# Holding the last three depths of two projections by token tile, in a fused transformer layer

## The chip, the core and the metric

The kernel runs on one core of one Trainium2 chip. The metric is the device time of one execution in microseconds (us), as the median of several; less is better. All arithmetic that matters is float32 in quality: the large matrix products are made from split operands, as told below.

## The reference

One encoder layer over 256 tokens of width 2048. What is computed, cut to what matters:

```
h = rms_norm(x, pre_mix_g);  z = h @ w_in                # 2048 -> 7296
ya = neighbourhood_attention(...)   # 512 columns
yb = rwkv7_mixer(...)               # 768 columns, a recurrence in both directions
yc = retention_mixer(...)           # 768 columns
y = concatenate([ya, yb, yc]) @ w_out[l]                 # 2048 -> 2048   "output projection"
x = x + rms_norm(y, post_mix_g[l])
h = rms_norm(x, pre_mlp_g[l])                            # "second norm"
u = square(relu(h @ w_up[l])) @ w_down[l]                # 2048 -> 8192 -> 2048, "up" and "down projection"
x = x + rms_norm(u, post_mlp_g[l])
```

All inputs are float32.

## The kernel before

**Splitting.** Every operand of a large product is split in two: a rounded high part and the rest. A product is then three matmuls: high by high, low by high, and high by low. ScalarE makes the high part of a weight half (`hi`, L1217 to L1221), VectorE its rest (`lo`, L692 to L697). A *half* is 128 partitions by 1024 weights, 512 KB. Halves are numbered h through the whole kernel: the input projection's, then the output projection's from OUT_H (32 halves, two for each of 16 depths of 128 rows), the up projection's from UP_H, the down projection's from DOWN_H (128 halves, two for each of 64 depths), up to END_H.

**Buffers.** The sync engine fetches half h into one of 4 raw slots when the rest of half h - 4 is made (`fetch`, L489). The split parts lie in a ring of 3 slots (`w_hi`, `w_lo`, SPLIT = 3). Both `hi(h)` and `lo(h)` therefore wait for the semaphore `gemm_half` to reach h - 2, which says that TensorE has finished half h - 3. The arena is a large tensor of 32,896 words for each partition, which holds everything else and is cut up anew in each stage.

**The output and down projections (`rows`, L1957 to L1997).** The stationary operand is a block of activations (128 rows of depth by 128 tokens), the moving one 512 weights. All 8 banks of PSUM are the accumulators: 4 for token tile 0, 4 for token tile 1, two for each half of the 2048 columns. A *part* (t, j) is 6 matmuls of 512 columns: one depth, one token tile t, one half j. For each depth: wait for half 2n, part (1, 0), part (0, 0), wait for half 2n + 1, part (1, 1), part (0, 1). The last depth goes in the order (0, 0), (0, 1), (1, 0), (1, 1), and each part signals on its own (`quarter_done`), so that the norm behind it can begin.

**The norm behind each of the two.** For each token tile and half ScalarE squares and sums (`half_squares`, L1498), and VectorE multiplies by the gain (`gained`, L1121); then come the root, its reciprocal, and two additions to x (`add_half`, L1136), each with its own signal. After the output projection those additions write `x1` (signal `x1_ready`), after the down projection the result, which goes out in 4 transfers.

**The second norm's blocks (`turned`, L1566; `split_h`, L685 on VectorE and L1210 on ScalarE).** x1 is transposed by TensorE in 16 blocks of two 128 by 128 transposes each, one block to a bank, in 6 banks; TensorE begins when three of the four additions are done (`least = 2 * TT - 1`). ScalarE makes the high part of a block out of PSUM, VectorE the rest, and from the seventh block on TensorE waits for the rest of the block six before. After all 32 transposes the up projection begins; depth kt of its first tile waits for the rest of block kt. The root of the second norm itself is applied after the up projection, from sums that ScalarE makes of x1.

**The down projection's activations.** ScalarE makes the high part of the activations of depth m (`u_split(m)`), then `hi` of its two halves. VectorE makes their rest (`u_rest(m)`), then `lo` of the two halves. TensorE waits for `ulo_done` of depth m before depth m.

**Before the output projection.** The mixers run in `turn(i)` for six retention heads; the first also finishes the recurrence's output: `summed_recurrence` (L1009) adds, `gated_recurrence` (L1014) multiplies, 128 by 1536 each. `gap()` is a place where the running input projection's work is put in: on TensorE its matmuls, on the others splits that they need. Then ScalarE copies 16 blocks of the mixed activations to their high parts (`head_of`) and VectorE makes their rests (`rest_of`). Both do blocks 0 and 1 first, then half OUT_H + 2, then all 14 other blocks in one go, and only then the further halves.

What sets the order: each engine has its own program written out by hand as above, and semaphores between them. Nothing is reordered at run time but by these waits.

## Time and profile before

| | us |
|---|---|
| median of 3 runs (1385.03 to 1386.26) | 1385.25 |
| the profiled execution, its own time | 1388.11 |
| span of its trace, first to last instruction | 1386.3 |
| TensorE busy (96%) | 1326.4 |
| VectorE busy (61%) | 840.1 |
| ScalarE busy (47%) | 646.0 |
| mean granted TensorE clock | 0.989 of full speed |

The 1.8 us between the span and the profiled execution's own time lie before the first and behind the last instruction. In the rows below, a timeline row is: start, duration, engine, line, operation, what it writes and reads, how many instructions are merged, and in square brackets the idle time before it with what ended it. PEld is TensorE's weight load. TensorE's matmul durations overlap one another, so the pace is read from the starts.

### The profile page before, as it was taken

The numbers are of one execution on the slowest core, as the hardware profiler recorded it, in microseconds if no ns is written. First come the engines' busy times: TensorE is split into PE (matmuls) and PEld (weight loads), VectorE is DVE, ScalarE is ACT, GpSimd is POOL, SyncE is SP. The second block draws the span as 40 slices with busy tenths as digits, with TensorE's granted clock in tenths as the row PEclk, the third lists the DMA queues.
The fourth block names the chain that finished last, engine by engine and source line by source line (L and its number), as shares of the span: only waits on it lengthen the run. The fifth ranks groups of instructions, "written<-read, shape, count | busy, mean of one in ns | idle before, by whom it ended". The sixth has DMA issues, their size and how long they took to land.

```text
span 1386.3 us, 25418 instructions
## 1 busy us (share of the span) xinstructions
PE 1326.4 (96%) x10537; PEld 1159.5 (84%) x10537; DVE 840.1 (61%) x1167; ACT 646.0 (47%) x983; POOL 299.2 (22%) x231
## 2 busy tenths in 40 slices
PE   6999999999999899898999999999999999999996
PEld 5999888888888899686888888888888888888885
DVE  5566788888876665545654554455455554555555
ACT  5465554455334345535544444444444444444443
POOL 0010223233315011000155555444440000000000
PEclk9999999999999999999999999999999999999999
DMA  8656333223339334485576666666666666666663
GB/s 246 185 163 189 104 90 93 78 78 92 102 99 213 92 107 120 139 285 155 147 218 183 185 188 189 184 186 190 185 185 194 197 191 192 195 195 191 192 196 122
DMA packets 285751, 226.50 MB, mean 163 GB/s; under 512 B 15237, under 2 KB 263301, under 8 KB 284741
## 3 DMA queue, kind: packets, MB, share of 16 engines
q1 hardware_dynamic: 285168, 223.64, 55.1%
q8 instruction: 83, 1.36, 0.4%
q0 software_dynamic: 240, 1.18, 0.3%
q14 instruction: 32, 0.25, 0.1%
q10 hardware_dynamic: 228, 0.07, 0.0%
HBM read 222.76 MB, written 2.10 MB: 162 GB/s over the span
## 4 chain that ended last, share of the span: by engine, by line
PE 84%; DVE 8%; ACT 5%; issue 2%; ACTq 0%; DVEq 0%
PE psum L1965 31%; PE psum L1605 17%; PE psum L1606 9%; PE psum L1594 7%; PE psum L1595 6%; PE psum L1596 6%; DVE w_lo L696 2%; PE psum L1734 1%; PE psum L1720 1%; ACT w_hi L1221 1%; DVE arena L865 1%; PE psum L1924 1%; PE psum L1811 0%; PE psum L1572 0%; PE psum L1932 0%
## 5 line engine op out<-in xcount | busy, mean ns | idle before, releaser
L696 DVE TENSOR_TENSOR w_lo<-raw,w_hi 128x1024 fp32r<-128x1024 f32 x402 | 505.4, 1260 | 444.4 <-ACT w_hi L1221 443.5
L1221 ACT ACTIVATE w_hi<-raw 128x1024 fp32r<-128x1024 f32 x402 | 424.5, 1059 | 489.5 <-PE psum L1965 233.2
L1605 PE MATMUL psum<-act_both,w_hi 128*128 128x512 f32 x1024 | 362.1, 399 | 0.0
L1965 PE MATMUL psum<-w_hi,act_both 128*128 128x512 f32 x1280 | 344.8, 391 | 5.7 <-DVE w_lo L696 2.6
L1965 PEld LDWEIGHTS psum<-w_hi,act_both 128*128 128x128 f32 x1280 | 240.5, 188 | 57.2 <-DVE w_lo L696 3.0
L1606 PE MATMUL psum<-act_both,w_lo 128*128 128x256 f32 x1024 | 287.6, 281 | 0.0
L1594 PE MATMUL psum<-act_both,w_hi 128*128 128x256 f32 x912 | 274.0, 300 | 3.9 <-DVE w_lo L696 2.4
L1595 PE MATMUL psum<-act_both,w_hi 128*128 128x256 f32 x912 | 259.8, 285 | 0.0
L1596 PE MATMUL psum<-act_both,w_lo 128*128 128x256 f32 x912 | 259.7, 285 | 0.0
L1605 PEld LDWEIGHTS psum<-act_both,w_hi 128*128 128x128 f32 x1024 | 192.4, 188 | 48.1 <-DVE w_lo L696 0.2
L1965 PE MATMUL psum<-w_lo,act_both 128*128 128x512 f32 x640 | 197.5, 390 | 0.0
L1606 PEld LDWEIGHTS psum<-act_both,w_lo 128*128 128x128 f32 x1024 | 193.4, 189 | 0.0
L1594 PEld LDWEIGHTS psum<-act_both,w_hi 128*128 128x128 f32 x912 | 176.2, 193 | 12.9 <-issue 5.2
L1595 PEld LDWEIGHTS psum<-act_both,w_hi 128*128 128x128 f32 x912 | 176.5, 194 | 0.3
L1596 PEld LDWEIGHTS psum<-act_both,w_lo 128*128 128x128 f32 x912 | 176.4, 193 | 0.0
L1965 PEld LDWEIGHTS psum<-w_lo,act_both 128*128 128x128 f32 x640 | 120.5, 188 | 25.1
L647 POOL TENSOR_TENSOR arena<-arena 128x512 f32<-128x512 f32 x32 | 42.4, 1325 | 304.8 <-DVE arena L1164 304.8
L650 POOL TENSOR_SCALAR arena<-arena 128x512 f32<-128x512 f32 x32 | 74.0, 2312 | 2.8
L652 POOL TENSOR_TENSOR arena<-arena 128x512 f32<-128x512 f32 x32 | 64.1, 2003 | 2.7
L640 POOL TENSOR_TENSOR arena<-arena 128x256 f32<-128x256 f32 x12 | 14.4, 1225 | 83.7 <-DVE arena L1024 83.7
L555 POOL TENSOR_TENSOR arena<-arena 128x256 f32<-128x256 f32 x12 | 10.7, 915 | 95.9 <-ACT arena L1316 95.9
L621 POOL TENSOR_SCALAR arena<-arena,small 128x64 f32<-128x64 f32 x24 | 16.2, 689 | 70.2 <-DVE arena L910 43.5
(201 smaller groups left out, 1055.5 us busy)
## 6 DMA issues: line engine op xcount, KB each, us to landing
raw<-in_w_up SPq DMA_DIRECT2D x128, 512.0 KB, 4.0
raw<-in_w_down SPq DMA_DIRECT2D x128, 512.0 KB, 4.5
raw<-in_w_in SPq DMA_DIRECT2D x114, 512.0 KB, 4.2
raw<-in_w_out SPq DMA_DIRECT2D x32, 512.0 KB, 4.5
arena<-in_x SPq DMA_DIRECT2D x2, 1024.0 KB, 6.5
arena<-in_na_rpb SPq DMA_DIRECT2D x16, 128.0 KB, 4.6
arena<-in_x SPq DMA_DIRECT2D x1, 2048.0 KB, 8.4
out_x<-arena SPq DMA_DIRECT2D x4, 512.0 KB, 2.7
```

The costliest lines, as they stand in the source:

```text
L621: last = pool.tensor_scalar(state_dec[:, d], state[:, d], ec[q][:, d, c:c + 1], None, ALU.mult)
L647: pool.tensor_tensor(r, r, token_scale.unsqueeze(1).broadcast_to([P, 2, T]), ALU.mult).then_inc(s["up_scaled"], 1)
L650: pool.tensor_scalar(r, r, 0.0, None, ALU.max).then_inc(s["up_scaled"], 1)
L652: pool.tensor_tensor(u[:, 2 * q:2 * q + 2], r, r, ALU.mult).then_inc(s["relu_free"], 1)
L696: dve.tensor_tensor(w_lo[:, h % SPLIT], raw[:, h % RAW], w_hi[:, h % SPLIT].bitcast(F32), ALU.subtract).then_inc(s["lo_half"], 1)
L1221: act.activation(w_hi[:, h % SPLIT], raw[:, h % RAW], ACT.Copy).then_inc(s["hi_half"], 1)
L1594: pe.matmul(dst, wh, act_hi[:, kt], start=kt == 0, stop=False)
L1595: pe.matmul(dst, wh, act_lo[:, kt], start=False, stop=False)
L1596: last = pe.matmul(dst, wl, act_hi[:, kt], start=False, stop=kt == KT - 1)
L1605: pe.matmul(bank[b].rearrange("p (a t) -> p a t", a=2), wh, act_both[:, :, kt], start=kt == 0, stop=False)
L1606: last = pe.matmul(bank[b][:, 0:T], wl, act_hi[:, kt], start=False, stop=kt == KT - 1)
L1965: last = pe.matmul(bank[4 * t + 2 * j + b], lhs[:, tokens], w[:, h % SPLIT, b * 512:(b + 1) * 512], start=start, stop=stop)
```

## The change

The last HELD = 3 depths of the output and of the down projection are done by token tile: first all their parts of token tile 0, then all those of token tile 1, with the split weights of all six halves kept. For this the last four halves of each projection get split slots of their own (`spare`), cut from the end of the arena. A helper `slot_free` says what a half waits for. The second norm's first twelve blocks are transposed two to a bank, in the order NORM_ORDER; four of them are begun for token tile 0 before token tile 1 is there. At the start of the output projection a weight half's split alternates with two activation blocks. In the mixers the two recurrence operations stand at other places. The core of the diff:

```diff
+HELD = 3
+        def spare_slot(h):
+            for end in (UP_H, END_H):
+                if end - 2 * HELD + 2 <= h < end:
+                    return h - (end - 2 * HELD + 2)
+            return None
+        def slot_free(eng, h):
+            if spare_slot(h) is not None:
+                eng.wait_ge(s["gemm_half"], h - 2 * HELD - 2)
+                eng.wait_ge(s["y_lo"], KT)
+            elif UP_H <= h < UP_H + 2:
+                eng.wait_ge(s["held_free"], h - UP_H + 1)
+            elif h == UP_H + 2:
+                eng.wait_ge(s["gemm_half"], UP_H - 2 * HELD)
+            elif h >= SPLIT:
+                eng.wait_ge(s["gemm_half"], h - SPLIT + 1)
+        NORM_ORDER = [0, 3, 1, 4, 2, 5, 6, 7, 9, 10, 8, 11, 12, 13, 14, 15]
+        NORM_EARLY = NORM_ORDER[:4]
+        def norm_place(k):
+            if k < 12:
+                return bank[2 + k // 6 * 3 + k % 3][:, k % 6 // 3 * T:(k % 6 // 3 + 1) * T]
+            return bank[k - 11][:, 0:T]
+        def norm_mate(k):
+            if k >= 12:
+                return k
+            return k + 3 if k % 6 < 3 else k - 3
 ...
@@ VectorE @@
                 rotate(i)
+                if i == 0:
+                    summed_recurrence()
                 gap()
 ...
-                    if i == 0:
-                        summed_recurrence()
                     gap()
                     take_p(i, 1)
                     if more:
                         maxima(i + 1)
-                    if i == 0:
-                        gated_recurrence()
                     gap()
                 decayed(i)
                 gap()
+                if i == 0:
+                    gated_recurrence()
 ...
-            lo(OUT_H + 2)
-            for n in range(2, KT):
+            for n in range(2, KT, 2):
+                lo(OUT_H + 1 + n // 2)
                 rest_of(n)
-            for h in range(OUT_H + SPLIT, UP_H + 1):
+                rest_of(n + 1)
+            for h in range(OUT_H + 1 + KT // 2, UP_H):
                 lo(h)
 ...
-            rs = gained(0, 1)
+            rs = gained(0, 1, lambda: lo(UP_H))     # lo(UP_H) between the two multiplications
 ...
+            def split_x1(blocks):
+                for k in blocks:
+                    dve.wait_ge(s["h_hi"], KT + k + 1)
+                    dve.scalar_tensor_tensor(act_lo[:, k], norm_place(k), vect("g2")[:, k:k + 1],
+                                             act_hi[:, k].bitcast(F32), ALU.mult, ALU.subtract).then_inc(s["h_lo"], 1)
+            split_x1(range(HALF_KT))
             lo(UP_H + 1)
-            split_h(("g2", KT))
+            split_x1(range(HALF_KT, KT))
             lo(UP_H + 2)
-            for t in range(TT):
-                token_root(t)
+            token_root(0)
+            lo(UP_H + 3)
+            token_root(1)
@@ ScalarE @@
+            out_square(0, 0, 0)
+            out_square(0, 0, 1)
+            hi(UP_H)
+            out_square(0, 1, 0)
+            hi(UP_H + 1)
+            x1_square(0, 0)
+            out_square(0, 1, 1)
+            x1_square(0, 1)
+            for k in range(KT):
+                act.wait_ge(s["xt_done"], KT + max(NORM_ORDER.index(k), NORM_ORDER.index(norm_mate(k))) + 1)
+                if norm_mate(k) < k:
+                    act.wait_ge(s["h_lo"], KT + norm_mate(k) + 1)
+                act.activation(act_hi[:, k], norm_place(k), ACT.Copy, scale=vect("g2")[:, k:k + 1]).then_inc(s["h_hi"], 1)
+            hi(UP_H + 2)
+            x1_square(1, 0)
+            hi(UP_H + 3)
+            x1_square(1, 1)
+            hi(UP_H + 4)
@@ TensorE @@
+            def held_rows(depths):
+                for n, lhs_hi, lhs_lo in depths:
+                    final = n == depths[-1][0]
+                    for j in range(2):
+                        pe.wait_ge(s["lo_half"], 2 * n + j + 1)
+                        last = part(n, lhs_hi, lhs_lo, 0, j, final=final)
+                        if final:
+                            last.then_inc(s["quarter_done"], 1)
+                for j in range(2):
+                    for n, lhs_hi, lhs_lo in depths:
+                        final = n == depths[-1][0]
+                        last = part(n, lhs_hi, lhs_lo, 1, j, final=final)
+                        if n == depths[0][0]:
+                            last.then_inc(s["held_free"], 1)
+                        elif final and j == 0:
+                            last.then_inc(s["quarter_done"], 1)
+                        elif final:
+                            last.then_inc(s["gemm_half"], 2 * HELD)
 ...
-            turned(x1, KT, "x1_ready", 2 * TT - 1)
+            pe.wait_ge(s["x1_ready"], 2)
+            for k in NORM_EARLY:
+                turn_x1(k, 0)
+            pe.wait_ge(s["x1_ready"], 3)
+            for n, k in enumerate(NORM_ORDER):
+                if k == 9:
+                    pe.wait_ge(s["x1_ready"], 4)
+                if k > 12:
+                    pe.wait_ge(s["h_lo"], KT + norm_mate(k - 13) + 1)
+                if k not in NORM_EARLY:
+                    turn_x1(k, 0)
+                turn_x1(k, 1).then_inc(s["xt_done"], 1)
 ...
-            for m in range(FF_T):
+            for m in range(FF_T - HELD):
                 pe.wait_ge(s["ulo_done"], m + 1)
-                rows(DOWN_H // 2 + m, u_hi[:, m % U_RING], u_lo[:, m % U_RING], m == 0, m == FF_T - 1)
+                rows(DOWN_H // 2 + m, u_hi[:, m % U_RING], u_lo[:, m % U_RING], m == 0)
+            pe.wait_ge(s["ulo_done"], FF_T)
+            held_rows([(DOWN_H // 2 + m, u_hi[:, m % U_RING], u_lo[:, m % U_RING])
+                       for m in range(FF_T - HELD, FF_T)])
```

The output projection's depths 13 to 15 go through the same `held_rows`, behind a wait for all 16 activation blocks.

## Rows read from the trace of the kernel before

**Rows 1.** Waits of TensorE over the whole run: total, times, longest.

```profile
PE psum L1572 <- DVE arena L1138: 6.7, 1, 6.7
...
PE psum L1965 <- DVE w_lo L696: 2.6, 1, 2.6
PE psum L1594 <- DVE w_lo L696: 2.4, 2, 1.8
```

**Rows 2.** Timeline of VectorE in the first mixer turn.

```profile
466.38 1.23 DVE L696 TENSOR_TENSOR w_lo<-raw,w_hi 128x1024 fp32r<-128x1024 f32 x1 [1.64 <-ACT w_hi L1221]
...
468.18 1.75 DVE L1009 TENSOR_TENSOR arena<-arena 128x1536 f32<-128x1536 f32 x1
...
473.03 1.76 DVE L1014 TENSOR_TENSOR arena<-arena 128x1536 f32<-128x1536 f32 x1
474.71 1.22 DVE L696 TENSOR_TENSOR w_lo<-raw,w_hi 128x1024 fp32r<-128x1024 f32 x1
```

**Rows 3.** Timeline at the output projection's start: TensorE, VectorE, ScalarE.

```profile
570.51 1.22 PE L1965 MATMUL psum<-w_hi,act_both 128*128 128x512 f32 x2 [2.58 <-DVE w_lo L696]
...
564.54 4.78 DVE L1106 TENSOR_TENSOR act_both<-arena,act_both 128x256 fp32r<-128x256 f32 x14
569.23 3.49 DVE L696 TENSOR_TENSOR w_lo<-raw,w_hi 128x1024 fp32r<-128x1024 f32 x3
...
562.26 4.39 ACT L1486 ACTIVATE act_both<-arena 128x256 fp32r<-128x256 f32 x14
```

**Rows 4.** Stretches: length, engines' busy time (instructions), granted clock, DMA share, GB/s.

```profile
570.50:573.90 3.40, 3.39 (x8) 2.72 (x9) 2.22 (x2) 0.00 (x0) 0.00 (x0) 0.50 0.63 188
...
651.40:655.80 4.40, 0.00 (x0) 0.00 (x0) 4.27 (x5) 4.30 (x10) 0.00 (x0) 1.00 0.02 5
655.80:662.60 6.80, 4.56 (x20) 3.96 (x21) 6.70 (x11) 5.64 (x13) 0.00 (x0) 0.50 0.11 31
...
590.00:610.00 20.00, 20.00 (x90) 16.57 (x89) 9.54 (x8) 7.42 (x7) 0.00 (x0) 1.00 0.91 341
```

**Rows 5.** Timeline of all engines from the output projection's end to the up projection.

```profile
656.68 2.48 DVE L1138 SCALAR_TENSOR_TENSOR arena<-arena,small 128x1024 f32<-128x1024 f32 x2
...
658.01 2.43 PEld L1572 LDWEIGHTS psum<-cst,arena 128*128 128x128 f32 x12 [7.08 <-DVE arena L1138]
658.02 6.81 PE L1572 MATMUL psum<-cst,arena 128*128 128x128 f32 x32 [6.66 <-DVE arena L1138]
...
659.81 5.95 ACT L1214 ACTIVATE act_both<-psum,vec 128x256 fp32r<-128x256 f32 x16 [1.13 <-PE psum L1572]
660.32 6.36 DVE L689 SCALAR_TENSOR_TENSOR act_both<-psum,vec,act_both 128x256 fp32r<-128x256 f32 x16
...
664.38 0.20 PEld L1572 LDWEIGHTS psum<-cst,arena 128*128 128x128 f32 x2 [0.19 <-DVE act_both L689]
...
664.58 0.48 PE L1605 MATMUL psum<-act_both,w_hi 128*128 128x512 f32 x1
```

**Rows 6.** Timeline late in the down projection: one step of its pipeline.

```profile
1356.75 1.06 ACT L1221 ACTIVATE w_hi<-raw 128x1024 fp32r<-128x1024 f32 x1 [1.66 <-PE psum L1965]
...
1357.85 1.23 DVE L696 TENSOR_TENSOR w_lo<-raw,w_hi 128x1024 fp32r<-128x1024 f32 x1 [1.49 <-ACT w_hi L1221]
...
1358.99 0.42 DVE L1173 TENSOR_TENSOR act_both<-arena,act_both 128x256 fp32r<-128x256 f32 x1
```

**Rows 7.** Timeline of the kernel's end.

```profile
1373.11 1.03 ACT L1501 ACTIVATE arena<-psum 128x1024 f32<-128x1024 f32 x1
...
1374.26 1.23 DVE L1130 TENSOR_TENSOR arena<-psum,arena 128x1024 f32<-128x1024 f32 x1
...
1375.17 0.61 PE L1965 MATMUL psum<-w_hi,act_both 128*128 128x512 f32 x2
...
1380.69 2.48 DVE L1138 SCALAR_TENSOR_TENSOR arena<-arena,small 128x1024 f32<-128x1024 f32 x2
```

**Rows 8.** The page's DMA issues for one weight: count, KB each, us from issue to landing.

```profile
raw<-in_w_down SPq DMA_DIRECT2D x128, 512.0 KB, 4.5
```

More of the change, by code:

```diff
@@ L202, in layer @@
         ARENA = 32896
-        arena = sb("arena", [P, ARENA])
+        LATER = ARENA - 2 * (2 * HELD - 2) * HALF
+        arena = sb("arena", [P, LATER])
+        with nc.sbuf_tensor("arena_later", [P, ARENA - LATER], F32) as arena_later:
+            pass
+        spare = sb("spare", [P, 2, 2 * HELD - 2, HALF], F32R)
+        spare_hi, spare_lo = spare[:, 0], spare[:, 1]
         psum = ctx.enter_context(nc.psum_tensor("psum", [P, 8, 512], F32))
@@ L458, in backwards, with high, low @@
                            ap=steps[:-1] + [[-last, count]])
+        def spare_slot(h):
[3 more added lines that the diff above has]
+            return None
+        def high(h):
+            return w_hi[:, h % SPLIT] if spare_slot(h) is None else spare_hi[:, spare_slot(h)]
+        def low(h):
+            return w_lo[:, h % SPLIT] if spare_slot(h) is None else spare_lo[:, spare_slot(h)]
+        def slot_free(eng, h):
[18 more added lines that the diff above has]
+            return k + 3 if k % 6 < 3 else k - 3
         def raw_landed(eng, h):
@@ L1121, in out_half, with gained @@
                 return psum[:, 4 * t + 2 * j:4 * t + 2 * j + 2].rearrange("p b n -> p (b n)")
-            def gained(stage, t):
+            def gained(stage, t, between=nothing):
                 rs = small[:, 200 + 16 * stage + t:201 + 16 * stage + t]
@@ L1164, in sum_halves @@
                 dve.tensor_tensor(r, halves[:, :, 1], r, ALU.add).then_inc(s["bank_free"], 1)
-            for h in range(UP_H + SPLIT, DOWN_H):
+            for h in range(UP_H + SPLIT + 1, DOWN_H):
                 lo(h)
@@ L1490, in _ @@
             gate_heads(RET_CT - 2, RET_CT)
-            hi(OUT_H + 2)
-            for n in range(2, KT):
+            for n in range(2, KT, 2):
+                hi(OUT_H + 1 + n // 2)
                 head_of(n)
-            for h in range(OUT_H + SPLIT, UP_H + 1):
+                head_of(n + 1)
+            for h in range(OUT_H + 1 + KT // 2, UP_H):
                 hi(h)
@@ L1532, in _ @@
-            for h in range(UP_H + SPLIT, UP_H + SPLIT + 2):
-                hi(h)
+                if t == TT - 1 and j == 1:
+                    act.wait_ge(s["gemm_half"], (UP_H, END_H)[stage])
+                else:
+                    act.wait_ge(s["quarter_done"], 3 * stage + 2 * t + j + 1)
+                half_squares(j, psum[:, 4 * t + 2 * j:4 * t + 2 * j + 2].rearrange("p b n -> p (b n)"),
+                             square_out[:, 0, t, j], base + 2 * t, small[:, base + 8 + t:base + 9 + t],
+                             TT * stage + t, "yss_done", "ypart_done", "yroot_done")
@@ L1561, in _, with turned @@
                 hi(DOWN_H + 2 * m + 1)
-            out_sums(1, END_H)
+            for t in range(TT):
+                for j in range(2):
+                    out_square(1, t, j)
         @block.tensor
         def _(pe):
-            def turned(src, first, ready, least=0):
+            def turned(src, first, ready):
                 def turn_block(k, t):
                     if k in (0, KT // 2):
-                        pe.wait_ge(s[ready], max(2 * t + 1 + k // (KT // 2), least))
+                        pe.wait_ge(s[ready], 2 * t + 1 + k // (KT // 2))
                     return pe.transpose(bank[2 + k % 6][:, t * P:(t + 1) * P], src[:, t, k * P:(k + 1) * P], ident)
@@ L1991, in rows @@
                         pe.wait_ge(s["lo_half"], 2 * n + 2)
-                    part(1, j)
+                    part(n, lhs_hi, lhs_lo, 1, j, first)
                     if first and j == 0:
                         pe.wait_ge(s["bank_free"], GROUPS + UP_GROUPS)
-                    part(0, j).then_inc(s["gemm_half"], 1)
-            for n in range(KT):
-                pe.wait_ge(s["y_lo"], n + 1)
-                rows(OUT_H // 2 + n, act_hi[:, OUT_ORDER[n]], act_lo[:, OUT_ORDER[n]], n == 0, n == KT - 1)
@@ L2001, in _ @@
-            turned(x1, KT, "x1_ready", 2 * TT - 1)
+                    part(n, lhs_hi, lhs_lo, 0, j, first).then_inc(s["gemm_half"], 1)
+            def held_rows(depths):
[6 more added lines that the diff above has]
+                            last.then_inc(s["quarter_done"], 1)
+                for j in range(2):
+                    for n, lhs_hi, lhs_lo in depths:
[7 more added lines that the diff above has]
+                            last.then_inc(s["gemm_half"], 2 * HELD)
@@ new lines, in _, with turn_x1 @@
+            for n in range(KT - HELD):
+                pe.wait_ge(s["y_lo"], n + 1)
+                rows(OUT_H // 2 + n, act_hi[:, OUT_ORDER[n]], act_lo[:, OUT_ORDER[n]], n == 0)
+            pe.wait_ge(s["y_lo"], KT)
+            held_rows([(OUT_H // 2 + n, act_hi[:, OUT_ORDER[n]], act_lo[:, OUT_ORDER[n]])
+                       for n in range(KT - HELD, KT)])
+            def turn_x1(k, t):
+                return pe.transpose(norm_place(k)[:, t * P:(t + 1) * P], x1[:, t, k * P:(k + 1) * P], ident)
```

79 lines of the change are left out of this document (28 added, 51 removed).

## The prediction

> **What bounds the kernel.** I read the page's busy shares first, then TensorE's waits, then the timeline around each wait that the diff touches, then the granted clock there. TensorE is busy in nearly all of the span, and the edits take no matmul away: 6 matmuls a part, as many parts, the same shapes, as many transposes. So time can only come from TensorE's idle time, from stretches at half clock, and from the tail after its last matmul. The waits show three places [rows 1]: 6.7 us before the second norm's transposes, 2.6 us in the output projection, and one of 1.8 us for a split in the mixers. The reader should see that VectorE is named as releaser in all three, although it is busy only 61% of the time: it is the order of its program that is late, not its speed.
>
> **Mixers.** The wait of 1.8 us ends with the split that starts at 474.71 us, and right ahead of this in VectorE's queue stands the multiplication of 1.76 us [rows 2]. The change puts that behind two splits. The sum of 1.75 us goes to a place where VectorE sat idle for 1.64 us ahead of the split at 466.38 us [rows 2]: it fits but for 0.1 us. Saved: 1.75 - 0.1 = 1.6 us. If something else is late next it is little, since attention's maxima, which stand between, then move forward with it. Bounds: 0 (another order-bound wait takes its place) to 1.8.
>
> **Start of the output projection.** TensorE waits 2.58 us for half OUT_H + 3, whose rest VectorE begins at 569.23 us, after 14 blocks in 4.78 us; ScalarE's 14 take 4.39 us from 562.26 us [rows 3]. In the new order ScalarE does two blocks (0.6 us) and then the high part: done at about 564.0; VectorE does two blocks from 564.5 (0.7 us) and then the rest: 565.2 to 566.4. TensorE needs it at 570.51 - 2.58 = 567.93, so 1.5 us early. The next halves follow at 2 us each (a rest of 1.2 and two blocks of 0.7), against 2.72 us that TensorE takes for a half (two parts of 1.36, the distance of successive parts at full clock). Nothing is late next. After this wait the granted clock stood at 0.50 for 3.4 us [rows 4], the lower of the two levels, 1.2 GHz: 3.4 us in which half the work was done, a loss of 1.7 us. TensorE had been idle for 2.6 us when it fell. Without the idle time I expect no fall. Saved: 2.6 + 1.7 = 4.3 us; bounds 2.6 (the clock falls there all the same) to 4.3.
>
> **Second norm.** Let T be the end of the output projection's last matmul, 658.02 - 6.66 = 651.36 us [rows 5]. Before, the up projection starts at 664.58, T + 13.2. Now token tile 0 is complete 6 parts, 8.2 us, ahead of T; its squares, table load, root and two additions end at about T - 2.6, all beside token tile 1's matmuls. Behind T only the last quarter is left. Its square starts at T; the multiplication by the gain comes 1.15 us after a square's start (1373.11 and 1374.26) [rows 7], so T + 1.2 to T + 2.4; the additions start at T + 2.65. Transposes waited before until 1.34 us after the start of the two additions (656.68 to 658.02 [rows 5]), hence now T + 4.0 instead of T + 6.7. The four early transposes lie in the idle time. 28 transposes are left. At the lower clock level 12 loads took 2.43 us, 0.20 each, and at the upper a pair 0.20, 0.10 each [rows 4, 5]: 5.7 or 2.8 us, so that TensorE alone could begin the up projection at T + 9.7 or T + 6.8. The others: ScalarE's first block comes some 0.8 us (0.5 at the upper level) after the transposes begin, VectorE's 0.5 us later, and a block costs 0.37 on ScalarE and 0.40 on VectorE [rows 5]. Eight rests, half UP_H + 1 (1.14), eight rests end at T + 13.3 (12.5). ScalarE's twelfth block waits for VectorE's ninth (a bank is shared), its sixteenth ends at T + 12.4 (11.7), then come the high part and the rest of half UP_H + 2, 1.1 and 1.2 us: T + 14.6 (13.9). TensorE needs that half 16 depths, 5.7 us, after it starts up: this binds like a start at T + 8.9 (8.2). The clock fell only 4.4 us after TensorE had gone idle here, and 2.6 us after it in the output projection [rows 4]; now it is idle for 3.1 us behind four short transposes, so either is possible. I take T + 8.9. Saved: 13.2 - 8.9 = 4.3 us; bounds 5.0 (upper level) and 2.7 (half clock also reaches into the up projection).
>
> **Supply of the held halves.** Token tile 0's six parts use up a half in 1.36 us instead of 2.72. The spare slots let the splits run ahead: half end - 5 is the last that waits for the ring. From its start, with 1.1 us for a high part, 1.14 us between rests [rows 6] and 4.5 us from issue to landing [rows 8], the rests of end - 4 to end - 1 are done 3.5, 4.8, 6.1 and 8.8 us later; TensorE wants them 5.4, 6.8, 8.2 and 9.5 us later. The last has 0.7 us to spare. I cost it at 0 in the output projection; bounds 0 to 1.
>
> **The down projection's held depths.** Here a new wait stands ahead of the held depths: all 64 rests of activations. VectorE does `u_rest(63)` only behind the rests of halves END_H - 5 to END_H - 3. Half END_H - 5 is still bound to the ring; its high part starts at 1356.75, its rest at 1357.85, `u_rest(62)` at 1358.99 [rows 6]. Then, 0.35 and 1.14 us on, the two rests at 1359.34 and 1360.48, `u_rest(63)` at 1361.62, and 0.42 us later, at 1362.05, TensorE may go. It finishes depth 60 at 1356.75 + 2.72 = 1359.47. A new stall of 2.6 us. Before, the same block was made 6 us early. Behind TensorE's wait stands its whole remaining program, so nothing covers it; only the weight supply gains. Whether the clock falls at this is open: an idle stretch of 2.58 us did it [rows 3, 4], in the second norm it took 4.4 us [rows 4], and this one comes after an unbroken run. Cost 0 or 1.7 us; I take half, 0.9.
> The row shows a fall in one case of about this length. The Trainium skill ("TensorE: Matmul & The Clock Gate", Part 1) says that half rate is the default which activity releases, and that the moment of change does not follow the kernel's start but an interval that runs freely. By that rule the fall would differ from run to run and from one version to the next; the sum would be 0.9 us lower or higher. No row here shows it twice at the same place.
>
> **The end.** Last matmul at 1375.17 + 0.61 = 1375.78, last addition done at 1380.69 + 2.48 = 1383.17: 7.4 us [rows 7]. Now, as in the second norm, square, multiplication, additions: 2.65 + 2.48 = 5.1 us. The table load lies beside matmuls. Saved 2.3 us. The last transfer behind it (3.1 us to the end of the span) stays. Bounds 2.0 to 2.4.
>
> **The sum**, on the profiled execution's own time of 1388.11 (span 1386.3 and 1.8 around it): - 1.6 - 4.3 - 4.3 + 2.6 + 0.9 - 2.3 = - 9.0, hence 1379.1. This execution lies 2.9 us above the median of the runs. The same difference on the median: 1385.25 - 9.0 = **1376.2 us**.
>
> **Rivals.**
> A. The stall ahead of the down projection's held depths does not show. For it: the splits run ahead into the spare slots. Against it: half END_H - 5 has none. Without 2.6 and 0.9: 1372.7.
> B. The second norm's start stays bound by the chain of blocks, with waits for banks shared in pairs in both directions, and the up projection starts 2.5 us later than I say, its first matmuls at half clock: 1378.7. For it: six cross-waits between three engines; against: each block costs only 0.4 us.
> C. The output projection's wait is replaced by another there (the alternate order makes activations late, or the clock falls all the same, with the mixers' 1.6 us lost too): 4.3 less saved, 1380.5. Against: 1.5 us of slack worked out above.
> D, slower than before. The supply does not double: in both held stretches token tile 0's six parts go at the old pace of 2.72 us. Price 6 x 1.36 = 8.2 us in each, of which the down projection's stall already covers 2.6: + 13.8, 1390.0. It takes back all of the 9.0 us once a half comes only every 1.36 + 9.0 / 12 = 2.1 us. For it: the raw ring is still 4 slots, and a landing takes 4.5 us. Against: between 590 and 610 us the DMAs moved 341 GB/s [rows 4], 1.54 us for a half, and two of the six are there ahead.
>
> **Chances.** My forecast 0.63, A 0.07, B 0.14, C 0.11, D 0.05. What a measurement of this kernel can tell from no change is about 0.2%, 2.8 us. Forecast, A, B and C are faster by more than that except for corners of B and C together with a clock fall: faster 0.92, within 0.04, slower 0.04. The likeliest's own range is 1374.5 to 1378; with A, most of B and C, and the clock's uncertain share of 1.7 us at three places, 1372.4 to 1380.2.
>
> **What would show it.** The wait for w_lo near 474 us is gone from the mixers. In the output projection no wait of over 0.5 us and no stretch at 0.50 behind 563 us. Transposes start 4.0 us after the last matmul of the output projection, and the up projection 8 to 9 us after it. One new wait of 2.6 us of L1965's successor on VectorE's `u_rest`, 16 us ahead of TensorE's end. The last addition 5.1 us after the last matmul. I am wrong if TensorE waits inside token tile 0's six parts, if the new wait is under 1 us, or if the up projection starts later than T + 10.5.

## The result, and the profile after

The changed kernel takes 1376.99 us (median of 20 runs, 1369.4 to 1379.3) against 1385.14 us for the kernel before (20 runs). The ratio is 0.9938, 95% interval 0.9928 to 0.9948: 8.6 us faster by the ratio, 8.2 by the two medians, where 9.0 were forecast. In one execution of each kernel in the later sets (2215.7 and 1627.3 us) the granted clock was far lower throughout, 0.64 and 0.75; the ratios leave such executions out. The profiled execution went from 1388.11 to 1378.10 us, and its span from 1386.3 to 1376.3.

| us | before | after |
|---|---|---|
| span | 1386.3 | 1376.3 |
| mean granted TensorE clock | 0.989 | 0.993 |
| first matmul of the output projection | 557.85 | 551.45 |
| its last matmul ends (T) | 651.36 | 642.60 |
| up projection starts | 664.58 (T + 13.2) | 650.33 (T + 7.7) |
| last matmul ends | 1375.78 | 1368.05 |
| last addition ends | 1383.17 (7.4 later) | 1373.17 (5.1 later) |

First the waits of TensorE over the whole run of the changed kernel, with total, times and longest. They answer to [rows 1].

```profile
PE psum L2084 <- DVE arena L1185: 3.5, 1, 3.5
...
PE psum L2029 <- DVE act_both L1229: 2.7, 1, 2.7
PE psum L2029 <- DVE act_both L1151: 2.2, 1, 2.2
PE psum L1945 <- DVE arena_later L1073: 2.1, 1, 2.1
...
PE psum L1660 <- DVE w_lo L741: 0.7, 1, 0.7
...
PE psum L1671 <- DVE w_lo L741: 0.5, 1, 0.5
...
PE psum L2029 <- DVE w_lo L741: 0.3, 1, 0.3
```

The wait of 6.7 us ahead of the transposes is now 3.5. The waits for a weight half of 2.6 and 1.8 us are gone. There is a new one of 2.7 us, for `u_rest` (L1229). One that the prediction did not touch grew: TensorE waits 2.1 us in the mixers for VectorE's copy L1073, where it had waited 1.6.

The mixers, to set beside [rows 2]: VectorE's timeline, with one row of GpSimd (POOL).

```profile
461.32 1.75 DVE L1054 TENSOR_TENSOR arena_later<-arena_later,arena 128x1536 f32<-128x1536 f32 x1
461.55 3.78 POOL L686 TENSOR_TENSOR arena_later<-arena,arena_later 128x256 f32<-128x256 f32 x2 [17.75 <-DVE arena_later L1069]
...
463.05 1.70 DVE L741 TENSOR_TENSOR w_lo<-raw,w_hi 128x1024 fp32r<-128x1024 f32 x1
...
464.76 0.65 DVE L1073 COPY arena_later<-psum 128x512 f32<-128x512 f32 x1
...
469.83 1.22 DVE L741 TENSOR_TENSOR w_lo<-raw,w_hi 128x1024 fp32r<-128x1024 f32 x1
470.97 0.75 DVE L1081 TENSOR_TENSOR arena<-psum,arena 128x256 f32<-128x256 f32 x2
471.63 1.75 DVE L1059 TENSOR_TENSOR arena_later<-arena_later,arena 128x1536 f32<-128x1536 f32 x1
```

The multiplication (L1059) now stands behind the split and the decay, and nobody waits for it. The sum (L1054) does fill the idle time, but the split behind it took 1.70 us instead of 1.23, and the copy L1073 comes 0.5 us later than before. In its new place the sum runs beside two multiplications of GpSimd (the next head's q and k), which had VectorE's idle time to themselves before:

```profile
464.89 1.43 POOL L640 TENSOR_TENSOR arena<-arena 128x256 f32<-128x256 f32 x2 [17.76 <-DVE arena L1024]
```

Together they took 3.78 us instead of 1.43, and the longer split lies in that time too. It is so in all 12 traces with the sum in its new place (3.78 or 3.79 us, split 1.70 or 1.71), and in neither of the two with the old one. That the two engines slow each other down is the obvious reading; no run separates them.

The second norm, TensorE, VectorE and ScalarE, to set beside [rows 5]:

```profile
642.45 0.60 PE L2084 MATMUL psum<-cst,arena 128*128 128x128 f32 x4
642.64 1.02 ACT L1557 ACTIVATE arena<-psum 128x1024 f32<-128x1024 f32 x1 [0.23 <-PE psum L2029]
...
643.79 1.23 DVE L1177 TENSOR_TENSOR arena<-psum,arena 128x1024 f32<-128x1024 f32 x1 [1.54 <-ACT arena L1557]
...
645.25 2.48 DVE L1185 SCALAR_TENSOR_TENSOR arena<-arena,small 128x1024 f32<-128x1024 f32 x2
...
646.59 3.99 PE L2084 MATMUL psum<-cst,arena 128*128 128x128 f32 x28 [3.54 <-DVE arena L1185]
...
650.33 0.48 PE L1671 MATMUL psum<-act_both,w_hi 128*128 128x512 f32 x1
...
655.40 1.23 DVE L741 TENSOR_TENSOR w_lo<-raw,w_hi 128x1024 fp32r<-128x1024 f32 x1 [0.27 <-ACT w_hi L1276]
...
656.68 0.50 PE L1671 MATMUL psum<-act_both,w_hi 128*128 128x512 f32 x1 [0.46 <-DVE w_lo L741]
```

From T = 642.60 on, the multiplication comes at T + 1.2, the additions at T + 2.65, the transposes at T + 4.0 and the up projection at T + 7.7. It then waits 0.46 us, from 656.22 on, for the rest of half UP_H + 2.

The down projection's held depths, which answer to [rows 6]:

```profile
1343.23 1.06 ACT L1276 ACTIVATE w_hi<-raw 128x1024 fp32r<-128x1024 f32 x1 [1.66 <-PE psum L2029]
...
1344.33 1.23 DVE L741 TENSOR_TENSOR w_lo<-raw,w_hi 128x1024 fp32r<-128x1024 f32 x1 [1.49 <-ACT w_hi L1276]
...
1345.47 0.42 DVE L1229 TENSOR_TENSOR act_both<-arena,act_both 128x256 fp32r<-128x256 f32 x1
1345.80 2.35 DVE L741 TENSOR_TENSOR spare<-raw,spare 128x1024 fp32r<-128x1024 f32 x2
...
1348.07 0.42 DVE L1229 TENSOR_TENSOR act_both<-arena,act_both 128x256 fp32r<-128x256 f32 x1
...
1348.55 1.22 PE L2029 MATMUL psum<-w_hi,act_both 128*128 128x512 f32 x2 [2.69 <-DVE act_both L1229]
```

It is the chain of the prediction: the rest of the last half bound to the ring, one rest of activations, two of weights, the last rest of activations, then TensorE.

Last the granted clock in stretches of the changed kernel (length, busy times of the engines, clock, DMA share, GB/s), beside [rows 4]:

```profile
475.90:479.30 3.40, 3.40 (x28) 3.24 (x27) 0.67 (x1) 2.52 (x6) 0.00 (x0) 1.00 0.50 148
552.40:555.80 3.40, 3.40 (x11) 2.57 (x10) 1.56 (x3) 3.36 (x5) 0.00 (x0) 0.53 0.02 7
...
646.60:650.30 3.70, 3.55 (x27) 2.93 (x28) 3.70 (x8) 3.24 (x9) 0.00 (x0) 1.00 0.00 0
1348.60:1354.50 5.90, 5.90 (x14) 4.64 (x15) 2.25 (x2) 1.06 (x1) 0.00 (x0) 0.50 0.02 10
```

**Where the 10.0 us between the two profiled executions came from**, by the distances of the marks above. The mixers' stretch starts at VectorE's L1021 (L1066 in the changed kernel), the down projection at the first `u_split`, at 1024.47 and 1010.94 us:

| part | us | made of |
|---|---|---|
| up to the first mixer turn | -3.3 | nothing that the change touches: most of it two stretches of 3.4 us at half clock fewer (1.7 each) |
| mixers | -3.1 | wait of 1.75 gone, 1.7 of half clock behind it gone, copy 0.5 later |
| output projection | -2.4 | wait of 2.6 gone with 1.7 of half clock; but 1.7 of half clock behind the old wait of 2.2, and a wait of 0.3 behind the load of x |
| T to the up projection's start | -5.5 | |
| up projection | +0.7 | 0.46 of it the wait for half UP_H + 2 |
| down projection | +5.8 | new wait 2.7, half clock behind it 3.1 |
| tail | -2.3 | |

The old wait of 1.75 us in the mixers had its stretch at half clock too, which I had not looked up. This is the kernel before:

```profile
478.30:481.70 3.40, 3.40 (x18) 3.40 (x18) 0.00 (x0) 1.84 (x9) 0.00 (x0) 0.51 0.84 241
```

### The profile page after: what moved, and what is told of

It reads as the page before. It is cut to its first block, busy times and chain, and to the rows that moved or that the text cites. A ratio compares the mean times of both kernels' runs of the same rounds, so it can differ in the third digit from the quotient of the medians.

```text
span 1376.3 us, 25419 instructions
## 1 busy us (share of the span) xinstructions
PE 1322.6 (96%) x10537; PEld 1156.5 (84%) x10537; DVE 840.7 (61%) x1167; ACT 646.3 (47%) x983; POOL 299.3 (22%) x231
## 4 chain that ended last, share of the span: by engine, by line
PE 83%; DVE 9%; ACT 5%; issue 2%; DMA 1%; ACTq 0%; DVEq 0%
PE psum L2029 31%; PE psum L1671 17%; PE psum L1672 9%; PE psum L1660 7%; PE psum L1661 6%; PE psum L1662 6%; DVE w_lo L741 2%; PE psum L1800 1%; ACT w_hi L1276 1%; DMA raw<-in_w_out 1%; PE psum L1786 1%; DVE arena L910 1%; PE psum L1990 1%; PE psum L1877 0%; PE psum L1727 0%
## 5 line engine op out<-in xcount | busy, mean ns | idle before, releaser
L741 DVE TENSOR_TENSOR w_lo<-raw,w_hi 128x1024 fp32r<-128x1024 f32 x394 | 497.0, 1264 | 419.9 <-ACT w_hi L1276 419.0
L1276 ACT ACTIVATE w_hi<-raw 128x1024 fp32r<-128x1024 f32 x394 | 416.4, 1059 | 470.5 <-PE psum L2029 214.9
L2029 PE MATMUL psum<-w_hi,act_both 128*128 128x512 f32 x1216 | 330.2, 392 | 6.1 <-DVE act_both L1229 2.7
L2029 PEld LDWEIGHTS psum<-w_hi,act_both 128*128 128x128 f32 x1216 | 229.7, 189 | 55.5 <-DVE act_both L1229 3.1
L2029 PE MATMUL psum<-w_lo,act_both 128*128 128x512 f32 x608 | 188.6, 392 | 0.0
L1660 PEld LDWEIGHTS psum<-act_both,w_hi 128*128 128x128 f32 x912 | 174.2, 191 | 11.2 <-issue 3.5
L2029 PEld LDWEIGHTS psum<-w_lo,act_both 128*128 128x128 f32 x608 | 115.0, 189 | 24.2
L686 POOL TENSOR_TENSOR arena_later<-arena,arena_later 128x256 f32<-128x256 f32 x12 | 15.7, 1328 | 79.3 <-DVE arena_later L1069 79.3
L601 POOL TENSOR_TENSOR arena<-arena 128x256 f32<-128x256 f32 x12 | 10.7, 911 | 95.9 <-ACT arena L1371 95.9
```

What stands on the lines that cost most here:

```text
L686: pool.tensor_tensor(qk_cos[:, n], src, late_const("cos"), ALU.mult).then_inc(s["rot_in"], 1)
L741: dve.tensor_tensor(low(h), raw[:, h % RAW], high(h).bitcast(F32), ALU.subtract).then_inc(s["lo_half"], 1)
L1276: act.activation(high(h), raw[:, h % RAW], ACT.Copy).then_inc(s["hi_half"], 1)
L1660: pe.matmul(dst, wh, act_hi[:, kt], start=kt == 0, stop=False)
L2029: last = pe.matmul(bank[4 * t + 2 * j + b], lhs[:, tokens], w[:, b * 512:(b + 1) * 512], start=start, stop=stop)
```

## The experiments

All times below are medians, and all ratios are to the kernel before in the same set, with 95% intervals. Its median was 1379.9, 1380.2 and 1382.8 us in the three sets. The changed kernel ran again in the second and third: 1371.5 us, ratio 0.9936 (0.9909 to 0.9964), and 1372.0 us, ratio 0.9932 (0.9909 to 0.9955). With these intervals the rounds tell 5 us, not 2; smaller things are read from the traces, stretch by stretch. The expectations of the first set are in us of the first comparison (1385 before, 1377 changed); with 1379.9 for the kernel before, only their distances to the changed kernel can be compared.

### The changed kernel again, twice

> The changed kernel itself once more, so that the others of this set are compared with it on one chip. Theory: the ratio to the kernel before is that of its first timing, 0.993 to 0.995 of it; the waits of TensorE are those of its first trace, and only the places where the granted clock falls differ. Rival (the gain was this one chip's): under 0.3% faster.

> The changed kernel once more, as the base of this set. The traces so far show two paces of the up projection, 2.77 and 2.83 us for a half, in kernels whose up projection is the same to the instruction, 6.6 us over its 128 halves. Theory (the pace belongs to an execution, not to a kernel): the times of this kernel fall in two groups about 6.5 us apart, near 1369 and 1376, in both kernels alike. Rival (chance falls of the clock of 1.7 us each make the spread): one group with steps of 1.7.

The ratios agree with the first. The waits are those of the first trace in both. The 11 times behind the third set's ratio are four from 1367.6 to 1368.9, three from 1371.5 to 1372.4 and four from 1376.1 to 1377.8; the 11 behind the second set's spread from 1366.9 to 1378.9 without clear groups. So the times alone show neither the two groups of the theory nor the rival's steps; that there are two paces is read from the traces (last section).

For the stall of the down projection, the trace of the second set gives the other outcome of the clock, and so does the third. One stretch, 1337.3 to 1350.0 us, holds the whole wait of 2.7 us and 10 us behind it, all at clock 1.00, where the first trace had 5.9 us at 0.50. The mixers have a stretch at half clock in this trace, behind the wait of 2.1 us for L1073, which the first and the third have not:

```profile
464.80:468.20 3.40, 3.40 (x15) 2.35 (x14) 1.74 (x2) 0.06 (x1) 0.00 (x0) 0.51 0.55 154
...
640.80:644.80 4.00, 0.46 (x5) 0.22 (x3) 2.75 (x4) 2.74 (x6) 0.00 (x0) 1.00 0.46 131
645.70:649.10 3.40, 3.40 (x18) 3.40 (x17) 3.40 (x10) 3.23 (x10) 0.00 (x0) 0.51 0.00 0
1337.30:1350.00 12.70, 10.01 (x44) 8.13 (x44) 6.68 (x8) 5.87 (x10) 0.00 (x0) 1.00 0.17 50
```

In the second norm it is the other way round: there the transposes ran at half clock, 28 loads in 4.70 us, and the up projection started at T + 8.7, now without a wait for half UP_H + 2:

```profile
643.43 2.48 DVE L1185 SCALAR_TENSOR_TENSOR arena<-arena,small 128x1024 f32<-128x1024 f32 x2
...
644.77 4.70 PEld L2084 LDWEIGHTS psum<-cst,arena 128*128 128x128 f32 x28 [3.78 <-DVE arena L1185]
...
649.47 0.47 PE L1671 MATMUL psum<-act_both,w_hi 128*128 128x512 f32 x1
```

So T + 8.2 (7.7 and the wait of 0.46) at the upper level and T + 8.7 at the lower one: the prediction had 8.2 and 8.9. The lower level is the common one, in 9 of the 11 traces with this norm. And the level costs nothing here: from T to the first `u_split`, 64 depths on, it is 368.3 us in the first trace (upper level) and 368.4 in two others (lower level) with the same pace of the up projection, against 373.1 before. The norm's gain is 4.7 to 4.8 us at either level.

### A wait for each held depth

```diff
-            pe.wait_ge(s["ulo_done"], FF_T)
             held_rows([(DOWN_H // 2 + m, u_hi[:, m % U_RING], u_lo[:, m % U_RING])
...
                 for n, lhs_hi, lhs_lo in depths:
+                    if n >= DOWN_H // 2:
+                        pe.wait_ge(s["ulo_done"], n - DOWN_H // 2 + 1)
                     for j in range(2):
```

> The changed kernel, but TensorE waits for the activations of each held depth of the down projection only before that depth, not for all 64 ahead of the first. Theory (the wait for all 64 is a stall of 2.69 us and pulls the clock down behind it for some 6 us, worth 3.1 us): no wait on the activations' rests 20 us before the end, granted clock 1.00 from there to the last matmul, and 2.7 to 5.8 us less than the changed kernel's 1377, so 1371 to 1374. Rival (the held depths are bound by the weight supply anyway, the wait only covers it): a wait for a weight half of over 1 us takes its place, and the time stays within 1 us of 1377.

> The wait for activations for each held depth, repeated. Theory: 2.7 us less than the changed kernel of this set in every execution, and up to 3.1 us more where the clock fell behind the stall there: about 3.5 us less, 0.25%. Rival (covered by supply): no difference.

First 1370.7 us, ratio 0.9929 (0.9904 to 0.9955), which is within 1 us or so of the changed kernel's ratio in the other sets; again 1366.2 us, 0.9888 (0.9857 to 0.9919), 5.7 us below the changed kernel of that set, more than the traces account for. The rounds alone would not settle this one; the traces do. The second trace:

```profile
1340.34 0.42 DVE L1229 TENSOR_TENSOR act_both<-arena,act_both 128x256 fp32r<-128x256 f32 x1
...
1340.68 5.60 PE L2029 MATMUL psum<-spare,act_both 128*128 128x512 f32 x24
```

TensorE passes through the held halves with no wait; the last `u_rest` ends at 1340.76, when TensorE has just begun the depth before the one that needs it. From the first `u_split` to the last matmul it takes 351.2 us in both traces, as the kernel before does (351.3), against 354.2 and 357.1 for the changed kernel without and with the clock's fall. The stall of 2.7 us is shown, and shown not to be covered: no wait for weights takes its place.

### The down projection not held

```diff
-            for end in (UP_H, END_H):
+            for end in (UP_H,):
...
-            for m in range(FF_T - HELD):
+            for m in range(FF_T - 1):
...
-            held_rows([(DOWN_H // 2 + m, u_hi[:, m % U_RING], u_lo[:, m % U_RING])
-                       for m in range(FF_T - HELD, FF_T)])
+            m = FF_T - 1
+            pe.wait_ge(s["lo_half"], END_H)
+            for t in range(TT):
+                for j in range(2):
+                    last = part(DOWN_H // 2 + m, u_hi[:, m % U_RING], u_lo[:, m % U_RING], t, j, final=True)
+                    if t == 1 and j == 1:
+                        last.then_inc(s["gemm_half"], 2)
+                    else:
+                        last.then_inc(s["quarter_done"], 1)
```

> The changed kernel with the down projection done as before (last depth only by token tile, no spare slots there), the output projection still held. Theory: the down part of the change costs more than it gives: 2.7 us of stall and up to 3.1 us of clock against 2.3 us of shorter tail. Without it 0.4 to 3.5 us less than the changed kernel: 1373.5 to 1376.6; last addition 7.4 us behind the last matmul. Rival (holding the down depths gains its 2.3 us in most runs): about 1379.

> The down projection not held, repeated. The first time it came out slower than the changed kernel had on another chip, against the theory that it would be faster. From the traces, step by step: no stall (2.7 less), no fall behind it (0 to 3.1 less), a longer tail (2.3 more): 0.4 to 3.5 us less than the changed kernel of this set. Rival: as the first time, 0.2% slower, which would need a cost of not holding that no trace shows so far.

1374.9 us, ratio 0.9960 (0.9941 to 0.9978), and again 1373.8 us, 0.9929 (0.9905 to 0.9952), beside 0.9932 for the changed kernel. The first came out as the rival said, the second level with the changed kernel; the rounds alone do not settle it. By the traces it is 351.3 us for the down projection in both and 7.4 us of tail, 358.7 together; the changed kernel takes 354.2 + 5.1 = 359.3 or 357.1 + 5.1 = 362.2, the kernel with a wait for each depth 356.3. So holding the down depths as the change does it costs 0.6 to 3.5 us more than it gives, and it gains 2.4 us once the wait is cut up. Why the first set showed it slower is not settled. Its profiled execution had the slower of two paces in the up projection (last section), 6.5 us more than the repeat's, which lies in no edit; a set with more such executions comes out slower, but only profiled executions show the pace.

### The mixers as before, and no alternation

```diff
-                if i == 0:
-                    summed_recurrence()
                 gap()
...
                     take_p(i, 0)
+                    if i == 0:
+                        summed_recurrence()
                     gap()
                     take_p(i, 1)
                     if more:
                         maxima(i + 1)
+                    if i == 0:
+                        gated_recurrence()
...
-                if i == 0:
-                    gated_recurrence()
```

> The changed kernel with the two recurrence operations of the mixers back in their old places. Theory: the wait of 1.75 us for a split near 474 us of the old trace comes back, with or without the fall of the clock that the old trace shows behind it (1.7 us): 1.3 to 3.4 us more than the changed kernel, 1378.3 to 1380.4. Rival (the wait was covered, something else was next): within 0.5 us of 1377.

1375.8 us, ratio 0.9967 (0.9946 to 0.9988), 4 us above what the changed kernel's ratio of the other sets gives. Its trace has the wait back, and from 477.7 us a stretch of 3.4 us at half clock behind it:

```profile
PE psum L1660 <- DVE w_lo L741: 2.4, 2, 1.8
```

From VectorE's L1066 to the first matmul of the output projection this trace takes 94.6 us, as the kernel before does (94.5). The 12 traces with the operations moved take 91.5 us in eight and 93.0 in four: in these four the clock falls behind the wait of 2.1 us instead. So the move is worth 3.0 or 1.5 us.

The second of the two edits, as VectorE's program has it; ScalarE's `hi` and `head_of` are put back in the same way:

```diff
-            for n in range(2, KT, 2):
-                lo(OUT_H + 1 + n // 2)
+            lo(OUT_H + 2)
+            for n in range(2, KT):
                 rest_of(n)
-                rest_of(n + 1)
...
```

> The changed kernel with the 14 activation blocks in one go again at the start of the output projection, all else as changed. Theory: the wait of 2.6 us for half OUT_H + 3 comes back, and 1.7 us at half clock behind it: 2.6 to 4.3 us more, 1379.6 to 1381.3. Rival (the clock falls there in either kernel, behind the 2.2 us wait that is left, so only the wait counts): 2.6 us or less.

1375.7 us, ratio 0.9975 (0.9956 to 0.9994), 5 us above the changed kernel's in the same sense. The wait is back, and so is the half clock behind it (from 568.7 us), besides another behind the wait of 2.2 us (from 555.1): both falls in one execution, against the rival.

```profile
PE psum L2027 <- DVE w_lo L741: 2.6, 1, 2.6
PE psum L2027 <- DVE act_both L1151: 2.2, 1, 2.2
```

These 4 and 5 us compare ratios taken on different chips, whose intervals overlap (the changed kernel's reach up to 0.9964), so the times only fit the theory; it is the traces that show the waits come and go with the edits.

### These two edits alone, on the kernel before

The diffs are those of the change for the mixers and for `hi`/`lo` beside `head_of`/`rest_of`, with nothing held.

> The kernel before with two of the four edits: the recurrence operations moved, and the alternation at the output projection's start. Nothing is held and nothing is transposed in pairs. Theory: these two take away 1.6 and 2.6 us of waiting and up to 1.7 us of half clock behind each: 4.2 to 7.6 us less than before, some 0.4%. Rival (most of the gain is the second norm's): under 3 us.

1376.5 us, ratio 0.9970 (0.9944 to 0.9996): 4.1 us, at the lower end. The changed kernel of the same set has 0.9936, so the two edits are about half of the whole, with an interval from nearly none to most of it; the second norm and the tail, less the new stall, are the rest. The trace has the norm as before, 6.7 us of wait and T + 13.2 to the up projection.

### Held, but one block to a bank

```diff
-        NORM_ORDER = [0, 3, 1, 4, 2, 5, 6, 7, 9, 10, 8, 11, 12, 13, 14, 15]
-        NORM_EARLY = NORM_ORDER[:4]
+        NORM_ORDER = list(range(KT))
+        NORM_EARLY = NORM_ORDER[:2]
...
-            if k < 12:
-                return bank[2 + k // 6 * 3 + k % 3][:, k % 6 // 3 * T:(k % 6 // 3 + 1) * T]
-            return bank[k - 11][:, 0:T]
+            return bank[2 + k % 6][:, 0:T]
...
-                return k + 3 if k % 6 < 3 else k - 3
+            return k
...
-                if k == 9:
+                if k == 8:
                     pe.wait_ge(s["x1_ready"], 4)
-                if k > 12:
-                    pe.wait_ge(s["h_lo"], KT + norm_mate(k - 13) + 1)
+                if k >= 6:
+                    pe.wait_ge(s["h_lo"], KT + k - 5)
```

> The changed kernel, depths held as there, but the second norm's blocks one to a bank in six banks in natural order, two begun early, each from the seventh on waiting for the rest of the block six before. Theory: TensorE begins transposes at the same 4.0 us after the output projection's end, but the last one waits for the tenth block's rest instead of the sixth's, and VectorE's half UP_H + 1 stands between the eighth and the ninth: the up projection begins at about T + 10.5 instead of T + 7.7, and its wait for half UP_H + 2 goes, so 2 to 2.5 us more than the changed kernel. Rival (pairing gains nothing, the chain of blocks binds both): same time within 0.5 us.

1374.6 us, ratio 0.9947 (0.9923 to 0.9971), 3.1 us above the changed kernel of its set, with overlapping intervals. In its trace T is at 642.64 + 1.07 = 643.71:

```profile
642.64 1.07 PE L2025 MATMUL psum<-spare,act_both 128*128 128x512 f32 x4
...
647.70 6.69 PE L2080 MATMUL psum<-cst,arena 128*128 128x128 f32 x30 [3.77 <-DVE arena L1181]
...
648.75 3.22 DVE L1201 SCALAR_TENSOR_TENSOR act_both<-psum,vec,act_both 128x256 fp32r<-128x256 f32 x8
...
651.89 1.22 DVE L737 TENSOR_TENSOR w_lo<-raw,w_hi 128x1024 fp32r<-128x1024 f32 x1
...
653.02 3.22 DVE L1201 SCALAR_TENSOR_TENSOR act_both<-psum,vec,act_both 128x256 fp32r<-128x256 f32 x8
...
654.14 0.48 PE L1667 MATMUL psum<-act_both,w_hi 128*128 128x512 f32 x1
```

The up projection starts at T + 10.4, with the last transposes waiting for the tenth rest, behind the weight half. The transposes ran at half clock here, and the changed kernel at half clock starts at T + 8.7: 1.7 us better. That is what the pairs in one bank, with their order, are worth; from T to the first `u_split` it is 1.7 to 2.0 us (363.8 against 361.8 to 362.1 in the traces of the same pace). The rest, 13.2 to 10.4, belongs to the token tiles' order together with the moves in ScalarE's and VectorE's programs that come with it; no run parts these two.

### Both repairs

The wait for each depth, and ScalarE's high part of half UP_H + 2 ahead of the norm's twelfth block:

```diff
             for k in range(KT):
+                if k == 11:
+                    hi(UP_H + 2)
                 act.wait_ge(s["xt_done"], KT + max(NORM_ORDER.index(k), NORM_ORDER.index(norm_mate(k))) + 1)
...
-            hi(UP_H + 2)
             x1_square(1, 0)
```

> The changed kernel with the wait for activations for each held depth of the down projection, and ScalarE's high part of half UP_H + 2 moved ahead of the second norm's twelfth block, where ScalarE waits 1.05 us for VectorE. Theory: the wait of 0.46 us for half UP_H + 2 shrinks by 0.3, as VectorE's rest then follows its last block at once; with the stall of 2.7 us gone some 3 to 6 us less than the changed kernel: 0.9895 to 0.9925 of the kernel before. Rival (the twelfth block comes later and delays VectorE's chain): the wait stays or grows, no more than the kernel with the wait for each depth alone.

> Wait for each depth and the early high part, repeated. Theory: as the kernel with the wait for each depth alone, less 0.3 to 0.5 us for the wait for half UP_H + 2, which the rounds can hardly tell: 3.5 to 4 us less than the changed kernel of this set. Rival: no better than that kernel.

1366.1 us, ratio 0.9902 (0.9866 to 0.9937), and 1366.6 us, 0.9889 (0.9860 to 0.9917). That is 1.0 to 1.1% below the kernel before, and 5.4 and 5.3 us below the changed kernel of the same set, where the intervals still overlap at their ends. It is no better than the wait for each depth alone (0.9888 in the second of these sets). The early high part itself is not shown to help: in both traces the transposes ran at half clock, in which case the changed kernel has no wait for half UP_H + 2 either; from T to the first `u_split` they take 362.1 us, and the kernels without it 361.8 to 362.1.

## Why the prediction was right, step by step

- **Mixers**, 1.6 forecast. The wait went as said. Two terms were mis-sized and nearly cancel: moving the sum costs 0.5 us, not 0.1 (the split behind it took longer), and I had not looked for the half clock behind that wait, 1.7 us, though the trace had it. Measured: 3.0 where the clock stays up, 1.5 where it falls behind the wait of 2.1 us that the move made longer (4 of 12 traces). The prediction thought that little could be late next; it was this.
- **Output projection**, 4.3 forecast, bound 2.6. The wait went with its half clock. But in the first trace the clock fell behind the old wait of 2.2 us, which it had not done before; for this one term that is the corner of rival C, and it left 2.4. In both repeats it stayed up there, and they gained 4.6.
- **Second norm**, 4.3 forecast with bounds 2.7 and 5.0, and 4.7 to 4.8 measured. Each mark came within 0.1 us up to the transposes. Behind them the time is partly luck. The prediction put TensorE's own transposes at T + 9.7 at the lower clock level and then took T + 8.9, set by half UP_H + 2; of two bounds the later one holds, so its own terms gave 9.7 and a gain of 3.5. Measured is T + 8.7, as only 3.4 us of the transposes ran at half clock and 28 loads took 4.70 us, not 5.7. Rival B, 2.5 us later, is out.
- **Supply of the held halves**, 0 forecast, and 0 it is. The wait of 0.3 us for a weight half in the first trace ends at 598.80 us, long before the held depths. Ahead of it, at 582.25 us, the load of x (2048 KB) and that of the gains (1024 KB) were issued between the halves, and ScalarE then waited 4.9 us for a half to land. Rival D is out: token tile 0's six parts in the down projection took 11.2 us with 5.9 of them at half clock, which is 8.2 at full clock.
- **The new stall**, 2.6 forecast at 1362.05 - 1359.47; 2.69 measured. Rival A is out. The clock's share, 0.9 as the mean of 0 and 1.7, has the mean right and the bound wrong. Over the six traces that have this stall it cost nothing in four, 1.6 us in one and 2.9 us in one (355.8 and 357.1 us for the down projection against 354.2): 0.8 us on the mean.
- **The end**, 2.3 forecast, 2.27 measured.

With the falls of the clock taken at their mean over the traces, the parts are 2.5 in the mixers, 3.7 in the output projection, 4.7 in the norm, 3.7 lost in the down projection and 2.3 at the end: 9.5 us, an estimate from one trace of the kernel before. The prediction had 1.6, 4.3, 4.3, 3.5 and 2.3. So the sum of 9.0 is right by its mechanism, and its closeness owes something to errors of 0.4 to 0.9 us that go both ways.

Single executions of one kernel differ mainly by where the granted clock falls and by the pace of the up projection. The profiled execution's gain of 10.0 us next to a forecast of 9.0 is partly luck, since 3.3 us of it lie ahead of every edit. The Trainium skill ("TensorE: Matmul & The Clock Gate", Part 1) says that the moment of change follows an interval that runs freely, and the traces agree: the same kernel, run again, had its half clock at other waits. No run tests that rule against another cause of such differences.

## What to carry to other kernels

Holding weights to reorder work by tile moves the wait to whatever else the held block needs: give each held depth its own wait, or the first one waits for inputs of the last. Where an engine other than the bound one is named as releaser although it is half idle, look at what stands ahead in its program; two such moves gave about half of this gain. Before you move work into an engine's idle time, look at what the other engines do in it: here GpSimd used that time, and the move cost 0.5 us instead of 0.1. With effects of a few us on a kernel whose executions differ by more, decide by distances between marks in the trace, and take two traces of each kernel.

## What the runs showed that I had not expected

**Two paces of the up projection.** Its 128 halves take 359.7 to 360.6 us from start to first `u_split` in five traces, and 353.2 to 354.1 in nine, at a granted clock of 1.00 in both, with the same instructions. ScalarE's high parts, each let go by TensorE, show it. The changed kernel in its first trace, starts 2.83 us apart:

```profile
906.35 1.06 ACT L1276 ACTIVATE w_hi<-raw 128x1024 fp32r<-128x1024 f32 x1 [1.77 <-PE psum L1672]
...
909.18 1.06 ACT L1276 ACTIVATE w_hi<-raw 128x1024 fp32r<-128x1024 f32 x1 [1.77 <-PE psum L1672]
```

and in its second, 2.77 us apart:

```profile
902.81 1.06 ACT L1276 ACTIVATE w_hi<-raw 128x1024 fp32r<-128x1024 f32 x1 [1.71 <-PE psum L1672]
...
905.58 1.06 ACT L1276 ACTIVATE w_hi<-raw 128x1024 fp32r<-128x1024 f32 x1 [1.71 <-PE psum L1672]
```

The changed kernel has both, and so has the one with the down projection not held; two of the chips have both too, with different kernels. So the pace belongs neither to a kernel nor to a chip; whether it changes between two executions of one kernel on one chip was not profiled. It is worth 6 to 7 us, most of what the whole change gains. The down projection, with 512 columns in every matmul, takes 351.2 to 351.4 us in each trace without a stall. What sets the pace was not found.

**The clock behind short waits.** Each stretch at half clock lasted 3.4 us, or twice that, in every trace, and cost at most half its length. (Those after the last matmul, where TensorE has no more work, aside.) How often one followed a wait:

| TensorE's wait | us | followed by half clock |
|---|---|---|
| mixers, for a split (1.6 us of wait shortly ahead of it) | 1.75 | 2 of 2 traces |
| mixers, for L1073 | 2.1 | 4 of 12 |
| ahead of the output projection | 2.2 | 5 of 14 |
| output projection, for half OUT_H + 3 | 2.6 | 2 of 2 |
| down projection's held depths | 2.7 | 2 of 6 |
| the changed kernel's second norm | 3.5 | 9 of 11 |

The length of the wait alone does not decide it.
